# Hybrid decoder step, second mixer: level evictions, level 0's exponentials and the eviction of value tiles take other places in the order

## The chip, the cores and the metric

The kernel runs on one core of a Trainium2 chip. The metric is the device time of one execution in microseconds (us), lower being better; the median of three runs is given. Inside the core, TensorE (PE) does the matmuls, VectorE (DVE) and ScalarE (ACT) the elementwise work, GpSimd (POOL) a few side tasks, and SyncE (SP) issues the DMA transfers. Each engine runs its own list of instructions strictly in the order in which the program writes them, and engines wait for each other by semaphores (`wait_ge`).

## The reference

Two layers over 544 tokens: a prompt of 512 tokens and 8 sampled sequences of 4 tokens, with 1024 features. Each layer is a half-step feed-forward block, a token mixer, another half-step feed-forward block and a gated embedding. Layer 0 mixes by GLA with 4 heads, layer 1 by HGRN2 with 8 heads; the second one is what changes here:

```python
def hgrn2_mixer(u, w_in, gn, w_out, lb, s0):
    z = u @ w_in
    q, f, i, g = jnp.split(z, cuts, axis=-1)
    q = jax.nn.silu(q)
    log_f = jnp.logaddexp(jnp.log(lb), jnp.log1p(-lb) + jax.nn.log_sigmoid(f))
    k = (1.0 - lb) * jax.nn.sigmoid(-f)
    o, s = chunked_gated_linear_recurrence(heads(q), heads(k), heads(i), heads(log_f), s0, 1.0)
    o = rms_norm(o, gn) * jax.nn.silu(heads(g))
    return o.reshape(B, T, HGRN_I_DIM) @ w_out, s
```

```python
attn = jnp.einsum('bthk,bshk,btshk->bhts', qc, kc, decay) * scale     # pairwise decay, s <= t
o_intra = jnp.einsum('bhts,bshv->bthv', attn, vc)
o_inter = jnp.einsum('bthk,bhkv->bthv', qc * jnp.exp(b), S) * scale
```

## The kernel before, in words

Weights come in units of 512 KB, through a ring of 4 slots (`w_raw`). ACT rounds a unit to its high part (`high`, L1136), DVE subtracts to get the low part (`low`, L1677), and PE multiplies high by high, high by low and low by high. `ahead(n)` on ACT and DVE prepares unit n + 2 while PE works on unit n. SP may load a slot again only when the unit in it is free; the units of the values are also read raw by `sample_values`, so the unit behind them waits for that too.

A mixer is worked in two groups of heads, one after the other. For the second mixer these are groups 2 and 3, of 4 heads each, and the steps of one group are:

- **features**: 8 tiles, keys j = 0 to 3 and queries j = 4 to 7, evicted by DVE (`head_out`). Behind them ACT and DVE make the gate: `gate_end` on DVE (L2141) leaves the log decay in `gate_sum` (G). The queries in Q get their swish on ACT (`queries`, L1377), heads 0 to 2 ahead of the unit that follows j = 7, and head 3 behind it.
- **steps**: PE runs gate tile g0 and the diagonal products `diagonal` (L804, which wait until both calls of `queries` are through: `q_made`), value unit v0, level 0, v1, level 1, v2, level 2, v3, level 3, gate tile g1, levels 4 and 5, gate tile g2 and level 6. The value units (L773) accumulate over v0 to v3 in four banks, one for each token tile.
- **levels**: the decayed attention inside a chunk of 128 is built from 7 levels of blocks of 1, 2, 4 ... 64 tokens. For level l DVE makes the differences of gates (`level_diffs`, L2031), ACT their exponential (L1424, `level_keys` on ACT) and the queries' one (L1408, `level_queries` on ACT), DVE the products with keys (L2059) and queries (L2087), PE the level's matmuls (`level`, L828), and DVE copies the result out of PSUM under a mask (`level_out`, L2010). `level_gates` (L2043) then adds up the gates for the next level. Levels 0 to 4 use the same PSUM banks, so PE's level l waits for the copy of level l - 1.
- **values**: ACT evicts the value tiles 0 to 3 and the samples' tile 4 with the row scale (`values_out`, L1386 and L1389). PE's g1 waits for tiles 0 and 1, its level 5 for tile 4, its g2 for all.
- **mix**: DVE multiplies the keys by their decay (L2165, `kdec_made`), SP then loads the second half of the samples' states, and PE's `sq` matmuls (L902) wait for these states.

What sets the order is only the order of the code of each engine. On PE the two waits that matter read:

```python
pe.wait_ge(s["q_made"], 2 * (gi - 1))                # diagonal
elif NH == 4 and l < 5: pe.wait_ge(s["lvl_out"], n)  # level
```

Of the kernel before, what the change touches and what calls it, by code (L numbers as in the profile page):

```python
# [154 lines left out]
def _build(nc, a, o, ctx):  # L155
# [99 lines left out]
    def gain_row(e):  # L255
# [12 lines left out]
        "lb_done gk_mm x_out x_made gate_abs gate_exp gate_ln ls_made c_made kx_made gd_made gd_abs gd_exp "  # L268
        "gd_ln k_made gate_made q_made kt_zero wup_zero k0_made diff_made ek_made eq_made kt_made qt_made lvl_mm lvl_out "
        "diag_mm diag_out xs_made vs_mm sdiag_out slvl_out chunk_exp qin_made ksuf_made ksuf_exp kdec_made dec_made "  # L270
        "kd_turned kds_turned vec_turned vec_made kd_out u_mm s_made kmask_made us_mm snew_made o_mm os_mm "
        "sq_mm sq_out ks_made seqmask_made os_out o_out osq_made var_mm var_ln ors_made og_pre og_silu og_made og_made_p out_hi out_lo ple_t ple_sig "
        "p_turned p_feat p_hi p_lo p_out ple_mm ple_x u_free y_even y_made y_turned ssq_turned y_out_a y_out_v"
    ).split()
    s = {n: ctx.enter_context(nc.semaphore(n)) for n in names}
# [278 lines left out]
    def _(pe):  # L554
# [205 lines left out]
        def values(gr, u, n):  # L760

            unit_ready(n)
            if u % 2:
                sample_values(gr, u, n)
            for c in range(4):
                if u == 0 and c == 0:
                    pe.wait_ge(s["feat_out"], gr.feat0 + gr.nfeat + 1)
                if u == 0 and c == 2 and gr.has_r:
                    pe.wait_ge(s["x_out"], 2)
                for k in range(2):  # L770
                    kk = 2 * u + k
                    for part, (x, w) in enumerate(((UH, WH), (UL, WH), (UH, WL))):
                        mm = pe.matmul(ps[:, V_BANKS[c], :], x[:, kk, c * P:(c + 1) * P], w[:, n % RING, k * 512:(k + 1) * 512],  # L773
                                       start=(kk == 0 and part == 0), stop=(kk == KT_D - 1 and part == 2))
            mm.then_inc(s["mm_units"], 1)

        def sample_values(gr, u, n):
# [347 lines left out]
    def _(act):  # L1125
# [207 lines left out]
        def features(gr):  # L1333
            n = gr.start
            for j in range(gr.nfeat):
                ahead(n)
                if j == 0 and gr.g == 0:
                    norm(gr.norm, True)
                if not gr.gla and j == 4:
                    gate(gr)  # L1340
                if not gr.gla and j == 6:
                    gate_end(gr)
                if not gr.gla and j == 7:
                    queries(gr, 0, 3)
                if gr.gi == 1 and j == 0:
                    gate(gr)
                n += 1
            if gr.gi == 0:
                gate(gr)
            for kind, j, levels in gr.steps[:-2]:  # L1350
                ahead(n)
                n += 1
                for lv in levels:
                    if lv == "diag":
                        if not gr.gla:
                            queries(gr, 3, 4)
                        level_queries(gr, 0)
                    elif lv and lv < 4:
                        level_keys(gr, lv)
                        level_queries(gr, lv)  # L1360
            level_keys(gr, 4)
            level_queries(gr, 4)
            values_out(gr, (0, 1))
            level_keys(gr, 5)
            level_queries(gr, 5)
            values_out(gr, (4, 2, 3))
            ahead(n)
            level_keys(gr, 6)
            level_queries(gr, 6)
            ahead(n + 1)  # L1370

        def queries(gr, h0, h1):

            act.wait_ge(s["feat_out"], gr.feat0 + 4 + h1)
            parts = [Q[:, h0 * T_PROMPT:h1 * T_PROMPT], Q[:, 4 * T_PROMPT + h0 * T_SAMPLE:4 * T_PROMPT + h1 * T_SAMPLE]]
            for q in parts:
                ins = act.activation(q, q, ACT.Silu)  # L1377
            ins.then_inc(s["q_made"], 1)

        def values_out(gr, tiles):  # L1380

            act.wait_ge(s["mm_units"], gr.v_unit + 4)
            act.wait_ge(s["rstd_done"], gr.norm + 1)
            for c in tiles:
                if c < 4:
                    ins = act.activation(V[:, c, :], ps[:, V_BANKS[c], :], ACT.Copy, scale=rstdT[:, c:c + 1])  # L1386
                else:
                    act.wait_ge(s["vs_mm"], 2 * gr.gi + 2)
                    act.activation(V[:, c, 0:P], ps[:, V_BANKS[c], 0:P], ACT.Copy, scale=rstdT[:, c:c + 1])  # L1389
                    for j in range(1, 4):  # L1390
                        rows = slice(32 * j, 32 * j + 32)
                        ins = act.activation(V[0:T_SAMPLE, c, j * P:(j + 1) * P], ps[rows, V_BANKS[c], 0:P], ACT.Copy,
                                             scale=rstdT[rows, c:c + 1])
                ins.then_inc(s["v_out"], 1)
# [277 lines left out]
    def _(dve):  # L1672
# [235 lines left out]
        def features(gr):  # L1908
            n = gr.start
            qs = [(Q, h, gr.q_scale if gr.gla else None) for h in range(gr.NH)]  # L1910
            ks = [(K, h, None) for h in range(gr.NH)]
            dests = ([(RT, None, None)] if gr.has_r else []) + (qs + ks if gr.gla else ks + qs)
            if gr.gi == 1:

                dve.wait_ge(s["x_out"], 4)
                dve.tensor_copy(halves(G[:, 0:2 * T_PROMPT]), OG[:, 6:8, 0:T_PROMPT])
                dve.tensor_copy(halves(samples(G, gr)), OG[:, 6:8, T_PROMPT:T]).then_inc(s["x_made"], 1)
                dve.wait_ge(s["x_made"], 1)
            for j, (dst, h, scale) in enumerate(dests):
                if not gr.gla and j == 5:  # L1920
                    log_sigmoid(gr)
                    gate(gr)
                    head_out(gr, j, n, dst, h, scale)
                    gate_diff(gr)
                    ahead(n)
                    gate_key(gr)
                    n += 1
                    continue
                if not gr.gla and j == 7:
                    gate_end(gr)  # L1930
                ahead(n)
                if gr.gi == 1 and j == 1:
                    log_sigmoid(gr)
                if gr.g == 1 and j == 0:
                    dve.wait_ge(s["og_made"], 2 * gr.gi)
                    dve.wait_ge(s["og_made_p"], 2 * gr.gi)
                if h is None:
                    feature_out(gr, j, n, dst)
                else:
                    head_out(gr, j, n, dst, h, scale)  # L1940
                n += 1
                if gr.g == 0 and j == 1:
                    sample_tokens(gr)
                if gr.g == 1 and j in (0, 2):
                    sequences(GROUPS[gr.gi - 1], j // 2)
                if gr.has_r and j >= gr.nfeat - 2:
                    gates_out(gr, range(2) if j == gr.nfeat - 2 else (2,))
            if gr.gi == 0:
                log_sigmoid(gr)
            for kind, j, levels in gr.steps[:-2]:  # L1950
                ahead(n)
                n += 1
                for lv in levels:
                    if lv == "diag":
                        if gr.gla:
                            level_gates(gr, 0)
                        feature_out(gr, gr.nfeat, n - 1, OG[:, 4 * gr.g, :])
                        if not gr.gla:
                            level_queries(gr, 0)
                            level_gates(gr, 0)  # L1960
                        if gr.has_r:
                            gates_out(gr, (3,))
                        diagonal(gr)
                        level_diffs(gr, 1)
                    elif lv and lv < 4:
                        level(gr, lv)
                        level_out(gr, lv - 1)
            level(gr, 4)
            level_out(gr, 3)
            level(gr, 5)  # L1970
            ahead(n)
            feature_out(gr, gr.nfeat + 1, n, OG[:, 4 * gr.g + 1, :])
            level_out(gr, 4)
            level_keys(gr, 6)
            if not gr.gla:
                level_queries(gr, 6)
            level_gates(gr, 6)
            if gr.gla:
                ahead(n + 1)
            else:  # L1980
                feature_out(gr, gr.nfeat + 2, gr.g3_unit - 1, OG[:, 4 * gr.g + 2, :])
# [78 lines left out]
                                        compact(DK, gr, L, r), ALU.mult)  # L2060
            ins.then_inc(s["kt_made"], 1)

        def level(gr, l):

            level_keys(gr, l)
            if not gr.gla:
                level_queries(gr, l)
            level_gates(gr, l)
            level_diffs(gr, l + 1)

        def level_queries(gr, l):

# [434 lines left out]
```

## Time and profile before

| | |
|---|---|
| median of three runs | 2236.64 us (2236.31 to 2238.49) |
| the profiled execution's own time | 2235.69 us |
| its span, first to last instruction | 2233.3 us |
| TensorE busy | 2213.9 us, 99% of the span |
| DVE, ACT, POOL busy | 1577.2 us, 1083.9 us, 332.3 us |
| granted TensorE clock, mean | 0.997 |

The span is what the rows below are read in; 2.4 us of the execution's own time lie outside it, and the median of the runs is 0.95 us above the profiled execution. A busy PE means that some matmul was in flight, so its gaps are the waits of PE, and a gap is what a change of order can take away or add.

### The profile page before, as it was taken

How to read it: one execution, taken by the hardware profiler on the slowest of the kernel's cores; microseconds unless marked ns; L12 is line 12 of the kernel's file. 1: busy time of each engine (PE TensorE's matmuls, PEld its weight loads, DVE VectorE, ACT ScalarE, POOL GpSimd, SP SyncE). 2: the span in 40 equal slices, each digit the busy share in tenths (PEclk: the TensorE clock that was granted, in tenths of full speed). 3: DMA queues.
4: the chain of work that ended last, by engine and by line, in shares of the span. 5: the costliest groups of instructions: out<-in, count | busy, mean ns of one | idle time of the engine just before them, and what ended most of it. 6: DMA issues, size and time to landing. Idle time of an engine off the chain costs nothing. (4 is left out here: it accounts for less than half of the span.)

```text
span 2233.3 us, 42317 instructions
## 1 busy us (share of the span) xinstructions
PE 2213.9 (99%) x17778; PEld 2168.5 (97%) x17778; DVE 1577.2 (71%) x2172; ACT 1083.9 (49%) x1573; POOL 332.3 (15%) x239
## 2 busy tenths in 40 slices
PE   9999999999999999999999999999999999999998
PEld 8999999989999999999999999998999999999998
DVE  7888833567678888535788884359688788886344
ACT  7555622443555555423655562255465565555234
POOL 3222101112111221000222210000000212220001
PEclk9999999999999999999999999999999999999999
DMA  4333333233352333333233333322333333333231
GB/s 136 102 107 95 102 100 83 58 105 93 102 137 76 107 102 102 91 102 86 67 110 99 95 100 95 105 71 67 91 95 105 104 91 95 111 97 107 83 96 49
DMA packets 387338, 213.36 MB, mean 96 GB/s; under 512 B 7007, under 2 KB 381438, under 8 KB 387150
## 3 DMA queue, kind: packets, MB, share of 16 engines
q1 hardware_dynamic: 386928, 210.59, 33.6%
q8 instruction: 140, 2.29, 0.4%
q14 instruction: 48, 0.39, 0.1%
q10 hardware_dynamic: 190, 0.05, 0.0%
q0 software_dynamic: 32, 0.03, 0.0%
HBM read 198.98 MB, written 11.67 MB: 94 GB/s over the span
## 5 line engine op out<-in xcount | busy, mean ns | idle before, releaser
L642 PE MATMUL ps<-u_diffs,w_high 128*128 128x272 f32 x2560 | 486.8, 288 | 2.3 <-DVE w_low L1773 1.7
L642 PEld LDWEIGHTS ps<-u_diffs,w_high 128*128 128x128 f32 x2560 | 402.1, 188 | 3.2 <-issue 3.0
L642 PE MATMUL ps<-u_diffs,w_low 128*128 128x272 f32 x1280 | 369.3, 289 | 0.0
L1677 DVE TENSOR_TENSOR w_low<-w_raw,w_high 128x1024 fp32r<-128x1024 f32 x205 | 259.1, 1281 | 98.1 <-ACT w_high L1136 97.8
L2399 POOL TENSOR_TENSOR hidden<-t_gate,t_up 128x544 f32<-128x544 f32 x84 | 190.1, 2263 | 717.7 <-ACT t_gate L1258 717.7
L570 PE MATMUL ps<-hid_high,w_high 128*128 128x272 f32 x1408 | 290.4, 287 | 0.0
L570 PE MATMUL ps<-hid_high,w_low 128*128 128x272 f32 x1408 | 289.5, 288 | 0.0
L570 PE MATMUL ps<-hid_low,w_high 128*128 128x272 f32 x1408 | 289.1, 287 | 0.0
L642 PE MATMUL ps<-u_high,w_low 128*128 128x272 f32 x960 | 277.5, 289 | 0.0
L642 PE MATMUL ps<-u_low,w_high 128*128 128x272 f32 x960 | 276.9, 288 | 0.0
L642 PE MATMUL ps<-u_high,w_high 128*128 128x272 f32 x960 | 275.9, 287 | 0.3 <-DVE w_low L1773 0.3
L1136 ACT ACTIVATE w_high<-w_raw 128x1024 fp32r<-128x1024 f32 x205 | 210.4, 1049 | 113.4 <-PE ps L570 73.6
L570 PE MATMUL ps<-u_high,w_high 128*128 128x272 f32 (+2 forms) x1168 | 245.7, 292 | 2.2 <-DVE u_low L1690 1.8
L642 PEld LDWEIGHTS ps<-u_diffs,w_low 128*128 128x128 f32 x1280 | 240.6, 188 | 0.0
L570 PE MATMUL ps<-u_high,w_low 128*128 128x272 f32 (+2 forms) x1168 | 240.4, 288 | 0.0
L570 PE MATMUL ps<-u_low,w_high 128*128 128x272 f32 (+2 forms) x1168 | 240.3, 287 | 0.0
L1773 DVE TENSOR_TENSOR w_low<-w_sums,w_high 128x512 fp32r<-128x512 f32 (+1 forms) x240 | 208.6, 869 | 21.5 <-ACT w_high L1227 20.5
L570 PEld LDWEIGHTS ps<-hid_low,w_high 128*128 128x128 f32 x1408 | 220.1, 188 | 0.0
L570 PEld LDWEIGHTS ps<-hid_high,w_low 128*128 128x128 f32 x1408 | 219.3, 188 | 0.0
L570 PEld LDWEIGHTS ps<-hid_high,w_high 128*128 128x128 f32 x1408 | 219.2, 188 | 0.0
L1161 ACT ACTIVATE u_high<-h_resid,vectors 128x544 fp32r<-128x544 f32 x48 | 36.1, 751 | 372.7 <-DVE h_resid L1873 322.3
L570 PEld LDWEIGHTS ps<-u_high,w_high 128*128 128x128 f32 x1168 | 184.1, 188 | 5.6 <-DVE u_low L1690 2.4
(292 smaller groups left out, 4093.7 us busy)
## 6 DMA issues: line engine op xcount, KB each, us to landing
w_raw<-in_ffn_w_gu_dram SPq DMA_DIRECT2D x176, 512.0 KB, 5.2
w_raw<-in_ffn_w_down_dram SPq DMA_DIRECT2D x64, 512.0 KB, 4.5
w_raw<-in_hgrn_w_in_dram SPq DMA_DIRECT2D x32, 512.0 KB, 4.7
w_raw<-in_gla_w_in_dram SPq DMA_DIRECT2D x25, 512.0 KB, 5.0
w_raw<-in_ffn_w_down_dram SPq DMA_DIRECT2D x32, 384.0 KB, 4.5
w_raw<-in_ple_w_gate_dram SPq DMA_DIRECT2D x16, 512.0 KB, 4.9
states_s<-in_state_gla_dram SPq DMA_DIRECT2D x8, 512.0 KB, 5.9
out_gla_s_dram<-states_s SPq DMA_DIRECT2D x8, 512.0 KB, 3.8
```

The costliest lines, as they stand in the source:

```text
L570: mm = pe.matmul(ps[:, bank + hf, 0:t1 - t0], weights(slot, w0 + k, wk, m0, P, kw), x[:, kk - w0, t0:t1], start=(kk == 0 and part == 0), s ...
L642: mm = pe.matmul(ps[:, bank, 0:HALF], half_slot(w, base, h)[:, k * P:(k + 1) * P], x(k), start=start and k == 0 and part == 0, stop=k == K ...
L1136: act.activation(WH[:, slot, :], RAW[:, slot, :], ACT.Copy).then_inc(s["hi_made"], 1)
L1161: act.activation(flat_of(UH, m), flat_of(H, m), ACT.Copy, scale=gain_of(e, m)).then_inc(s["uh_done"], 1)
L1677: dve.tensor_tensor(WL[:, slot, :], RAW[:, slot, :], WH[:, slot, :].bitcast(F32), ALU.subtract)\
L1773: dve.tensor_tensor(half_slot(WL, base, h, n), src, half_slot(WH, base, h, n).bitcast(F32), ALU.subtract)\
L2399: pool.tensor_tensor(HID[:, f, :], tG[:, :], tU[:, :], ALU.mult).then_inc(s["hid_mul"], 1)
```

## The change

On DVE, for the second mixer: level 0's gate sums and level 1's differences are issued behind the last query tile, ahead of the weights' low part, the gate tile's eviction and the diagonal's. `level_out` of level l - 1 stands ahead of `level_gates` of level l, where it stood behind `level_diffs` of level l + 1. On ACT, for the second mixer: level 0's exponentials and its copy of the keys are issued ahead of the queries' swish, and value tiles 0 and 1 are evicted ahead of level 4's exponentials. On PE: a new semaphore `v_mm` is raised behind token tiles 0 and 1 of the last value unit, and ACT's eviction of these two tiles waits for it, in both mixers, where it waited for the whole unit. No instruction that computes is added or removed.

```diff
@@ values (PE) @@
+                if u == 3 and c < 2:
+                    mm.then_inc(s["v_mm"], 1)
             mm.then_inc(s["mm_units"], 1)
@@ features (ACT) @@
                 if not gr.gla and j == 7:
+                    level_queries(gr, 0)
                     queries(gr, 0, 3)
...
                     if lv == "diag":
-                        if not gr.gla:
+                        if gr.gla:
+                            level_queries(gr, 0)
+                        else:
                             queries(gr, 3, 4)
-                        level_queries(gr, 0)
...
+            if not gr.gla:
+                values_out(gr, (0, 1))
             level_keys(gr, 4)
             level_queries(gr, 4)
-            values_out(gr, (0, 1))
+            if gr.gla:
+                values_out(gr, (0, 1))
@@ values_out (ACT) @@
-            act.wait_ge(s["mm_units"], gr.v_unit + 4)
             act.wait_ge(s["rstd_done"], gr.norm + 1)
             for c in tiles:
+                if c < 2:
+                    act.wait_ge(s["v_mm"], 2 * gr.gi + c + 1)
+                else:
+                    act.wait_ge(s["mm_units"], gr.v_unit + 4)
@@ features (DVE) @@
                     head_out(gr, j, n, dst, h, scale)
+                if not gr.gla and j == 7:
+                    level_gates(gr, 0)
+                    level_diffs(gr, 1)
...
                             level_queries(gr, 0)
-                            level_gates(gr, 0)
...
                         diagonal(gr)
-                        level_diffs(gr, 1)
+                        if gr.gla:
+                            level_diffs(gr, 1)
                     elif lv and lv < 4:
                         level(gr, lv)
-                        level_out(gr, lv - 1)
             level(gr, 4)
-            level_out(gr, 3)
-            level(gr, 5)
+            level(gr, 5, False)
@@ level (DVE) @@
-        def level(gr, l):
+        def level(gr, l, out=True):
             level_keys(gr, l)
             if not gr.gla:
                 level_queries(gr, l)
+                if out:
+                    level_out(gr, l - 1)
             level_gates(gr, l)
             level_diffs(gr, l + 1)
+            if gr.gla and out:
+                level_out(gr, l - 1)
```

On ACT, group 2, from the unit's high part behind j = 7 to the keys' exponential of level 1 (`q<-q` is the swish, `ex<-gate_sum` and `k_tilde<-k` are level 0's exponentials and copy), before:

```order
L1136 ACTIVATE w_high<-w_raw 128x1024
L1377 ACT_TABLE_LOAD
L1377 ACTIVATE q<-q 128x1536
L1377 ACTIVATE q<-q 128x96
L1136 ACTIVATE w_high<-w_raw 128x1024
L1377 ACTIVATE q<-q 128x512
L1377 ACTIVATE q<-q 128x32
L1406 ACT_TABLE_LOAD
L1406 ACTIVATE ex<-gate_sum 128x64
L1408 ACTIVATE ex<-gate_sum 128x8x64 x2
L1416 ACTIVATE k_tilde<-k 128x512 x2
L1136 ACTIVATE w_high<-w_raw 128x1024 x2
```

and now, in the same place (lines have moved by 2 to 10):

```order
L1138 ACTIVATE w_high<-w_raw 128x1024
L1416 ACTIVATE ex<-gate_sum 128x64
L1418 ACTIVATE ex<-gate_sum 128x8x64 x2
L1426 ACTIVATE k_tilde<-k 128x512 x2
L1384 ACT_TABLE_LOAD
L1384 ACTIVATE q<-q 128x1536
L1384 ACTIVATE q<-q 128x96
L1138 ACTIVATE w_high<-w_raw 128x1024
L1384 ACTIVATE q<-q 128x512
L1384 ACTIVATE q<-q 128x32
L1138 ACTIVATE w_high<-w_raw 128x1024 x2
L1434 ACT_TABLE_LOAD
```

The three groups of level 0 moved ahead of the swish; the number of table loads is the same, and the second one now stands ahead of level 1's exponential.

On DVE, group 2, levels 3 and 4 (`w_low` is a unit's low part, `k_tilde` and `q_tilde` the level's keys and queries, `gate_sum` the gate sums, `ex` the next level's differences, `attn` the copy under the mask), before:

```order
L1677 TENSOR_TENSOR w_low<-w_raw,w_high 128x1024
L2059 TENSOR_TENSOR k_tilde<-k,ex 128x64x8 x2
L2087 TENSOR_TENSOR q_tilde<-q,ex 128x8x64 x2
L2043 TENSOR_TENSOR gate_sum<-gate_sum 128x8x8x8 x2
L2031 TENSOR_TENSOR ex<-gate_sum 128x8x64 x2
L2010 COPY_PREDICATED attn<-masks,ps 128x8x16x4 x2
L2059 TENSOR_TENSOR k_tilde<-k,ex 128x32x16 x2
```

and now:

```order
L1687 TENSOR_TENSOR w_low<-w_raw,w_high 128x1024
L2070 TENSOR_TENSOR k_tilde<-k,ex 128x64x8 x2
L2102 TENSOR_TENSOR q_tilde<-q,ex 128x8x64 x2
L2021 COPY_PREDICATED attn<-masks,ps 128x8x16x4 x2
L2054 TENSOR_TENSOR gate_sum<-gate_sum 128x8x8x8 x2
L2042 TENSOR_TENSOR ex<-gate_sum 128x8x64 x2
L2070 TENSOR_TENSOR k_tilde<-k,ex 128x32x16 x2
```

The copy moved two places up, so that the differences of level 4 now stand directly ahead of the keys of level 4, which need the exponential of these differences.

## Rows read from the trace of the kernel before

**Rows 1.** The page's busy times: engine, busy us, share of span, instructions.
```profile
PE 2213.9 (99%) x17778; PEld 2168.5 (97%) x17778; DVE 1577.2 (71%) x2172; ACT 1083.9 (49%) x1573; POOL 332.3 (15%) x239
```

**Rows 2.** Waits of PE over the whole span: total us, times, longest.
```profile
PE ps L828 <- DVE attn L2010: 2.8, 4, 1.0
```

**Rows 3.** Timeline of PE, group 2: start, duration, instruction, idle before and releaser.
```profile
1512.52 3.73 PE L804 MATMUL ps<-q,k 128*128 128x128 f32 x32
...
1530.43 0.40 PE L773 MATMUL ps<-w_low,u_high 128*128 128x512 f32 x1
1531.84 2.02 PE L828 MATMUL ps<-q_tilde,k_tilde 128*128 128x128 f32 x16 [1.01 <-DVE attn L2010]
...
1539.57 0.40 PE L773 MATMUL ps<-w_low,u_high 128*128 128x512 f32 x1
1540.36 2.02 PE L828 MATMUL ps<-q_tilde,k_tilde 128*128 128x128 f32 x16 [0.40 <-DVE attn L2010]
...
1556.75 3.73 PE L828 MATMUL ps<-q_tilde,k_tilde 128*128 128x128 f32 x32
...
1581.62 1.96 PE L902 MATMUL ps<-states_s,q 128*32 128x128 f32 x64 [0.27 <-issue]
```

**Rows 4.** Timeline of ACT, group 2.
```profile
1506.66 1.04 ACT L1136 ACTIVATE w_high<-w_raw 128x1024 fp32r<-128x1024 f32 x1
1507.72 1.28 ACT L1377 ACT_TABLE_LOAD   x1
...
1511.53 0.73 ACT L1377 ACTIVATE q<-q 128x512 f32<-128x512 f32 x2
...
1513.57 0.26 ACT L1406 ACTIVATE ex<-gate_sum 128x64 f32<-128x64 f32 x1
...
1516.02 1.99 ACT L1136 ACTIVATE w_high<-w_raw 128x1024 fp32r<-128x1024 f32 x2
...
1529.82 1.06 ACT L1136 ACTIVATE w_high<-w_raw 128x1024 fp32r<-128x1024 f32 x1 [6.06 <-DMA w_raw<-in_hgrn_w_in_dram]
...
1552.62 1.06 ACT L1424 ACTIVATE ex<-ex 128x1024 f32<-128x1024 f32 x1 [2.17 <-DVE ex L2031]
1553.58 1.14 ACT L1408 ACTIVATE ex<-gate_sum 128x512 f32<-128x512 f32 x2
1554.98 1.11 ACT L1392 ACTIVATE v_tok<-ps,rstd_tok 32x128 f32<-32x128 f32 x3
```

**Rows 5.** Timeline of DVE, group 2.
```profile
1504.96 3.39 DVE L2141 SCALAR_TENSOR_TENSOR gate_sum<-gate_sum,lbd,gate_tmp 128x512 f32<-128x512 f32 x8 [1.08 <-ACT gate_tmp L1463]
...
1537.71 2.50 DVE L2010 COPY_PREDICATED attn<-masks,ps 128x512 f32<-128x512 uint32 x2
...
1552.50 1.33 DVE L2010 COPY_PREDICATED attn<-masks,ps 128x512 f32<-128x512 uint32 x2
1553.81 1.29 DVE L2059 TENSOR_TENSOR k_tilde<-k,ex 128x512 f32<-128x512 f32 x2
1555.02 1.28 DVE L2087 TENSOR_TENSOR q_tilde<-q,ex 128x512 f32<-128x512 f32 x2
1556.23 1.28 DVE L2043 TENSOR_TENSOR gate_sum<-gate_sum 128x512 f32<-128x512 f32 x2
1557.55 1.29 DVE L2031 TENSOR_TENSOR ex<-gate_sum 128x512 f32<-128x512 f32 x2
1558.76 1.22 DVE L1677 TENSOR_TENSOR w_low<-w_raw,w_high 128x1024 fp32r<-128x1024 f32 x1
...
1566.51 0.72 DVE L1881 TENSOR_TENSOR out_gate<-ps,rstd 128x544 f32<-128x544 f32 x1 [1.06 <-PE ps L570]
...
1571.83 2.49 DVE L2165 TENSOR_TENSOR k<-k,ex 128x1024 f32<-128x1024 f32 x2
```

**Rows 6.** Waits of SP's queue, 1565 to 1590 us.
```profile
SPq L477 <- DVE k L2165: 4.0, 1, 4.0
```

**Rows 7.** Windows, PE in the first mixer: stretch, its us, busy, granted clock.
```profile
598.00:603.00 5.00, 5.00 (x23) 0.66 0.00 0
```

More of the change, by code:

```diff
@@ L270, in _build @@
         "diag_mm diag_out xs_made vs_mm sdiag_out slvl_out chunk_exp qin_made ksuf_made ksuf_exp kdec_made dec_made "
-        "kd_turned kds_turned vec_turned vec_made kd_out u_mm s_made kmask_made us_mm snew_made o_mm os_mm "
+        "kd_turned kds_turned vec_turned vec_made kd_out u_mm v_mm s_made kmask_made us_mm snew_made o_mm os_mm "
         "sq_mm sq_out ks_made seqmask_made os_out o_out osq_made var_mm var_ln ors_made og_pre og_silu og_made og_made_p out_hi out_lo ple_t ple_sig "
```

## The prediction

> **What bounds the kernel now.** I read the page's busy times first. PE is busy for 99% of the span [rows 1], so the time is PE's work plus its few waits, and off PE's path a shorter wait is worth nothing. Then PE's waits: the only ones in the second mixer that this change is near are the four ahead of the levels' matmuls (L828), which wait for DVE's masked copies (L2010), 2.8 us in all [rows 2]. The timeline of PE in group 2 shows two of them, 1.01 us ahead of level 1 and 0.40 us ahead of level 2 [rows 3]; four waits in two groups that run the same code make the other two group 3's. The reader is to see what a wait really costs: the matmuls of v1 start 0.23 us apart, so behind the one at 1530.43 level 1 could start at 1530.66 and started at 1531.84, 1.18 us late; behind the one at 1539.57 level 2 started at 1540.36 where 1539.80 was possible, 0.56 us late. That is 1.74 us a group, 3.5 us for both: the most that the change can win on this path, 0.16% of the time.
>
> Then I followed what PE waits for just ahead of that, whether or not it waits long: the diagonal (L804) needs both swish calls (`q_made`). On ACT the last swish starts at 1511.53 and takes 0.73, so ends at 1512.26 [rows 4]; PE's diagonal starts at 1512.52 [rows 3]. No idle time is shown there, but the slack is 0.26 us and no more.
>
> **The change, part by part.** I take group 2 and write its schedule on with the durations of the rows. A handover between DVE and ACT takes some 0.04 us; from DVE to PE it is 0.15.
>
> *Swish later.* On ACT, the unit's high part at 1506.66 ends at 1507.70. There the table load and the swish followed; now level 0's exponentials come first. They need the gate: DVE's L2141 group starts at 1504.96 and takes 3.39, to 1508.35 [rows 5]. So ACT idles for 0.7 us, to 1508.39, and then does the exponentials and the key copy, which took from 1513.57 to 1516.02, 2.45 us [rows 4]. Everything up to the last swish moves by 0.69 + 2.45 = 3.14, and `q_made` comes at 1515.40. No cover: PE has issued g0 and stands at the diagonal, with 0.26 us of slack. With the handover it starts at 1515.55, **3.0 us later than before**. Behind PE's waiting instruction stands all of PE's work, so the whole of it moves.
>
> *DVE's sums earlier, copies earlier.* With PE 3.0 us later, level 1 can start at 1530.66 + 3.03 = 1533.69. DVE now has 2.7 us less to do ahead of the copy of level 0 (gates and differences at 1.3 each [rows 5], the samples' small ones aside), and a PE that comes later: the copy ends about 1530, and PE doesn't wait. Level 2 could start 7.9 us after level 1, at 1541.6; what DVE needs for it is below, and it is ready at about 1540. So both old waits go: the balance at level 2 is 1541.6 against 1540.36, **+1.2 us**.
>
> *What is late next: levels 4 and 5.* DVE is held at one place by a transfer. The high part of g1's weights waited for its DMA until 1529.82 [rows 4]; SP may only issue it when `sample_values` of v1 is through, so it moves with PE, to 1532.85, the high part ends at 1533.91, and DVE's low part starts at 1533.95. From there I add starts on DVE [rows 5]: low part 1.15; level 2's keys 1.2, queries 1.2, copy 2.45, gates 1.3, differences 1.2; low part 1.2; level 3's five the same but with a copy of 1.3, 6.2. That is 1549.85. Before, the copy stood between the differences of level 4 and the keys of level 4, and it covered the time that ACT takes for the exponential between them (1.06 us, L1424 [rows 4]). Now nothing stands there: DVE waits 1.2 us (1.06, two handovers and the tail of the differences). Level 4 6.2, again a wait of 1.2, keys and queries of level 5 2.5: 1560.95 to 1561.05. Levels 1 to 3 don't show this bubble, since the next unit's low part stands in the same place. PE reaches level 5 half of its 3.73 us behind the start at 1556.75 [rows 3], moved by 1.2, so at 1559.7, and starts at 1561.2: **+1.45 us**. ACT gives the same figure: value tile 4, which level 5 needs too, comes behind the exponentials of level 5, which start at 1557.5; exponentials 2.0 and tile 1.4 end it at 1560.9.
>
> *Value tiles one by one.* Tiles 0 and 1 now go out while PE still does tiles 2 and 3. ACT has them done before level 4's differences reach it, so this costs nothing; it wins nothing either, since PE's g1 shows no wait for them before. In the first mixer only the semaphore changes, and PE shows no idle row in its levels there.
>
> *The states.* From the gates of level 5 to the end of the keys' decay, before, DVE took from 1556.23 to 1574.32, with 1.06 us idle [rows 5]: 17.0 us of work. Now it starts at 1561.0 and has no idle time left: 1578.1, 3.8 us later. SP loads the second half of the states behind that (its 4.0 us wait for L2165 [rows 6]), and PE's L902, which needs them, started at 1581.62, behind an idle of 0.27 us put down to "issue" [rows 3]. I take this to be the landing, 7.3 us behind the keys' decay. It comes at 1585.4 now, while PE, moved by 1.2 + 1.45 and about 0.2 more at level 6, would be there at 1584.3. So **+0.9 us**, and group 2 ends 3.8 us later. If the landing is not what held L902, this term is nothing.
>
> *Sum.* Group 2 gives +3.8. Group 3 runs the same code; I have no row of a wait at its L902, so its landing came up to 0.3 us earlier, and I take +3.6, between 3.0 without that term and 3.8. Together **+7.4 us**: the profiled execution's span of 2233.3 becomes 2240.7, its own time of 2235.69 becomes 2243.1, and the median, 0.95 above that execution, 2244.0. PE has no later wait in which this could vanish: its remaining waits are for copies and sums that move with it.
>
> *The clock.* In the first mixer, from 598 to 603, the granted clock is 0.66 on average, one fall to half (1.2 GHz) and back, behind a stretch of small matmuls with no idle row [rows 7]. It takes 5.0 x 0.34 = 1.7 us of clock. The wait at the diagonal is three times the longest one that the second mixer now has. The Trainium skill (TensorE: Matmul & The Clock Gate, "Why this matters for your kernels") advises against long gaps between bursts of matmuls, since an idle PE falls back to half its clock; by that rule each diagonal would bring a slow stretch. The trace does not show it for a gap of this length, only the fall in the first mixer. By the row the sum stays at 2244.0; by the rule it would be 3.4 more.
>
> **The rivals.** *The clock falls behind the diagonal's wait* in one or both groups: 2245.7 or 2247.4. For it: the fall of [rows 7] needed no idle row at all. Against: the waits of 1.01 us cost none, and the work on both sides is dense. *Only the swish counts*: DVE keeps up better than I add up (the transfer of g1 lands early, or the bubble is filled), levels 5 and 6 and the states cost nothing, and each group ends 1.2 us later: 2239.0, within what can be told from no change. For it: the added terms stand on a chain of some 25 starts, and 1.4 us of slack would hide them. Against: each start is a row. *The swish is not late*, the other side: the change does what its order suggests, the two waits go and nothing comes, -3.5 us, 2233.1. This needs `q_made` to be at most 0.26 us later than before. It decides on the 0.7 + 2.45 us on ACT; it turns into a loss when ACT's delay passes 0.26 + 1.74 = 2.0 us. Against it: both figures are rows, and ACT went from the high part into the swish's table load without a gap [rows 4], so there is no idle time in front of it to fill. *The change doesn't do what it says*: the copies wait for PE's level 0 anyway, so moving them up is worth less than their 2.7 us; but with PE late the old waits go in any case, so this leaves the sum as it is.
>
> **How the numbers follow.** A measurement of this kernel can tell about 0.2%, 4.5 us, from no change, so faster begins at 2232.2 and slower at 2241.1. My forecast with its near variants (2242 to 2245): 0.55. The clock in one or both groups: 0.20. Only the swish: 0.14. The swish not late: 0.06, of which a third ends beyond 0.2%. Something between: 0.05. So slower 0.79 (0.55 + 0.20 and most of what lies between), same 0.18, faster 0.03. Likeliest 2244.0; the range for 8 in 10 reaches down to the case of the swish alone and up to both slow stretches: 2238.8 to 2248.0. The likeliest case's own range is 2242 to 2246.
>
> **What would show it.** Right: PE idle for about 2.8 us ahead of the diagonal in both groups, released by ACT's swish; no wait for L2010 ahead of levels 1 and 2; a wait of about 1.3 us ahead of level 5, released by the queries or value tile 4; DVE idle for 1.2 us ahead of the keys of levels 4 and 5; L902 up to 1 us late behind its states. Wrong: a diagonal without a wait, which would throw the whole sum; or the diagonal's wait with none ahead of level 5, which leaves +1.2 us a group. A stretch of half clock behind the diagonal would show the first rival.

## The result and the profile after

| | before | after |
|---|---|---|
| median | 2236.47 us (2235.13 to 2238.49, 6 runs) | 2245.4 us (2242.05 to 2247.53, 6 runs) |
| profiled execution, own time | 2235.69 us | 2245.68 us |
| its span | 2233.3 us | 2243.9 us |

The ratio is 1.0038, 95% interval 1.0027 to 1.0048: slower by 8.9 us, clear of the 0.2% that can be told. The forecast was 2244.0, with 2238.8 to 2248.0 for 8 in 10. Of all executions on record one, in the second set of runs of the changed kernel, was slow throughout (2389.57 us at a mean granted clock of 0.85), and no figure below holds it.

The timeline of PE after, with the places that answer to [rows 3]: the diagonal, levels 1, 2, 4 and 5 and the states' matmuls of group 2, then diagonal, level 5 and states of group 3:

```profile
1515.33 5.43 PE L806 MATMUL ps<-q,k 128*128 128x128 f32 x32 [2.93 <-issue]
...
1535.18 1.95 PE L830 MATMUL ps<-q_tilde,k_tilde 128*128 128x128 f32 x16
...
1543.07 1.95 PE L830 MATMUL ps<-q_tilde,k_tilde 128*128 128x128 f32 x16
...
1559.38 1.95 PE L830 MATMUL ps<-q_tilde,k_tilde 128*128 128x128 f32 x16
1562.62 2.02 PE L830 MATMUL ps<-q_tilde,k_tilde 128*128 128x128 f32 x16 [1.30 <-DVE q_tilde L2102]
...
1586.89 1.95 PE L904 MATMUL ps<-states_s,q 128*32 128x128 f32 x64 [1.16 <-issue]
...
1660.50 3.81 PE L806 MATMUL ps<-q,k 128*128 128x128 f32 x32 [2.90 <-issue]
...
1706.36 2.02 PE L830 MATMUL ps<-q_tilde,k_tilde 128*128 128x128 f32 x16 [1.49 <-DVE q_tilde L2102]
...
1729.92 1.96 PE L904 MATMUL ps<-states_s,q 128*32 128x128 f32 x64 [0.45 <-issue]
```

The diagonal now has 2.93 and 2.90 us of idle time in front of it, where it had none. Levels 1 and 2 start without a wait. Level 5 waits for DVE's queries, and L904 (L902 before) waits in both groups. The diagonal of group 2 also takes 5.43 us for what takes 3.81 in group 3: the clock.

```profile
1510.00:1525.00 15.00, 12.07 (x72) 0.89 0.00 1
1655.00:1670.00 15.00, 12.10 (x80) 1.00 0.01 1
```

These are windows of PE after (stretch, its us, busy, granted clock, DMA share, GB/s), 15 us around the two diagonals: the first has a stretch at half clock, the second has none, with the same idle time.

The changed kernel was profiled once more later. Its rows of the diagonal, level 5 and the states in both groups:

```profile
1515.24 5.33 PE L806 MATMUL ps<-q,k 128*128 128x128 f32 x32 [2.92 <-issue]
...
1562.30 2.02 PE L830 MATMUL ps<-q_tilde,k_tilde 128*128 128x128 f32 x16 [1.16 <-DVE q_tilde L2102]
...
1586.26 1.96 PE L904 MATMUL ps<-states_s,q 128*32 128x128 f32 x64 [0.86 <-issue]
...
1659.84 3.81 PE L806 MATMUL ps<-q,k 128*128 128x128 f32 x32 [2.88 <-issue]
...
1705.52 2.02 PE L830 MATMUL ps<-q_tilde,k_tilde 128*128 128x128 f32 x16 [1.30 <-DVE q_tilde L2102]
...
1728.58 1.95 PE L904 MATMUL ps<-states_s,q 128*32 128x128 f32 x64
```

The diagonals are as in the first profile, the slow first one included, and level 5 waits in both groups; but group 3's states are waited for in the first profile only.

The timeline of ACT after, which answers to [rows 4]:

```profile
1506.38 1.05 ACT L1138 ACTIVATE w_high<-w_raw 128x1024 fp32r<-128x1024 f32 x1
1508.12 0.26 ACT L1416 ACTIVATE ex<-gate_sum 128x64 f32<-128x64 f32 x1 [0.68 <-DVE gate_sum L2156]
...
1510.69 1.28 ACT L1384 ACT_TABLE_LOAD   x1
...
1514.50 0.73 ACT L1384 ACTIVATE q<-q 128x512 f32<-128x512 f32 x2
...
1534.21 1.06 ACT L1138 ACTIVATE w_high<-w_raw 128x1024 fp32r<-128x1024 f32 x1 [13.40 <-DMA w_raw<-in_hgrn_w_in_dram]
```

The reader is to see the wait of 0.68 us for the gate, and that the swish's table load comes 4.3 us behind the start of the high part, where it came 1.06 behind it. The last swish ends at 1515.23 and PE's diagonal starts at 1515.33: so I take "issue" in PE's row to be this semaphore; a run further down, with less idle time there, names it (`<-ACT q L1386`).

The timeline of DVE after, which answers to [rows 5]:

```profile
1504.68 3.40 DVE L2156 SCALAR_TENSOR_TENSOR gate_sum<-gate_sum,lbd,gate_tmp 128x512 f32<-128x512 f32 x8 [1.08 <-ACT gate_tmp L1473]
...
1552.57 1.29 DVE L2070 TENSOR_TENSOR k_tilde<-k,ex 128x512 f32<-128x512 f32 x2 [1.22 <-ACT ex L1434]
...
1560.03 1.29 DVE L2070 TENSOR_TENSOR k_tilde<-k,ex 128x512 f32<-128x512 f32 x2 [1.23 <-ACT ex L1434]
1561.24 1.29 DVE L2102 TENSOR_TENSOR q_tilde<-q,ex 128x512 f32<-128x512 f32 x2
...
1571.58 0.73 DVE L1891 TENSOR_TENSOR out_gate<-ps,rstd 128x544 f32<-128x544 f32 x1
...
1576.89 2.50 DVE L2180 TENSOR_TENSOR k<-k,ex 128x1024 f32<-128x1024 f32 x2
```

The two bubbles ahead of the keys of levels 4 and 5 are there, 1.22 and 1.23 us; the idle time that DVE had ahead of the gate tile's eviction is used up; the keys' decay ends at 1579.39, where it ended at 1574.32.

### The profile page after: what moved, and what is told of

The parts are those of the page before. It is cut to its first block, busy times and chain, and to the rows that moved or that the text cites. A ratio compares the mean times of both kernels' runs of the same rounds, so it can differ in the third digit from the quotient of the medians.

```text
span 2243.9 us, 42317 instructions
## 1 busy us (share of the span) xinstructions
PE 2216.8 (99%) x17778; PEld 2172.0 (97%) x17778; DVE 1575.7 (70%) x2172; ACT 1084.5 (48%) x1573; POOL 332.7 (15%) x239
## 4 chain that ended last, share of the span: by engine, by line
PE 93%; DVE 3%; ACT 2%; issue 1%; DMA 0%; POOL 0%; DVEq 0%; ACTq 0%; SPq 0%
PE ps L570 46%; PE ps L642 37%; PE ps L773 3%; PE ps L830 1%; PE ps L890 1%; PE ps L806 1%; PE ps L924 1%; PE ps L871 1%; PE ps L956 0%; DVE attn L2021 0%; DMA w_raw<-in_hgrn_w_in_dram 0%; PE ps L970 0%; DVE w_low L1783 0%; DVE ex L2042 0%; PE ps L940 0%
```

## The experiments

Three theories stand in the expectations. A is that of the prediction: the late swish, the gap that the copies left open, and the states behind them. B: the swish is the whole loss. C: the early copies are. Each set of runs stands beside runs of the kernel before on the same chip. To compare places across runs that start a little apart, I count from the start of DVE's gate end (the L2141 group of [rows 5]) of the same group to the diagonal and to L902, and from group 2's gate end to the first matmul of the output projection. Times that a run's own clock falls add are in these numbers.

| kernel | ratio to before, 95% interval | group 2: diagonal, L902 | group 3: diagonal, L902 | to projection |
|---|---|---|---|---|
| before | 1 | 7.56, 76.66 | 7.57, 76.33 | 230.18 |
| changed | 1.0038 (1.0027, 1.0048) | 10.65, 82.21 | 10.63, 80.05 | 239.46 |
| swish first | 1.0023 (1.0014, 1.0033) | 7.55, 78.18 | 7.59, 77.59 | 234.59 |
| level 0 alone | 1.0036 (1.0023, 1.0048) | 10.65, 80.13 | 10.65, 78.74 | 238.81 |
| copies 2, 3 late | 1.0020 (1.0011, 1.0028) | 10.61, 80.09 | 10.61, 77.59 | 236.53 |
| both repairs | 0.9993 (0.9984, 1.0002) | 7.56, 75.70 | 7.59, 75.79 | 230.30 |
| states split | 1.0042 (1.0030, 1.0055) | 10.63, 79.06 | 10.60, 80.90 | 237.15 |
| wait filled (12) | 1.0029 (1.0018, 1.0041) | 10.60, 79.40 | 10.59, 80.29 | 236.88 |
| changed, second set | 1.0035 (1.0024, 1.0046) | 10.63, 81.65 | 10.61, 79.35 | 239.81 |
| both repairs, states split | 0.9997 (0.9989, 1.0006) | 7.56, 75.43 | 7.58, 75.75 | 229.38 |
| tiles together | 1.0055 (1.0041, 1.0069) | 10.62, 81.62 | 10.63, 80.36 | 240.81 |
| tiles together, second set | 1.0043 (1.0029, 1.0057) | 10.62, 81.89 | 10.61, 82.32 | 242.19 |
| tiles together, wait filled | 1.0027 (1.0016, 1.0039) | 10.59, 79.99 | 10.59, 80.11 | 237.31 |

**Swish first.** The changed kernel with level 0's exponentials and sums put back:

```diff
 # ACT, features
-                    level_queries(gr, 0)
                     queries(gr, 0, 3)
...
-                        if gr.gla:
-                            level_queries(gr, 0)
-                        else:
+                        if not gr.gla:
                             queries(gr, 3, 4)
+                        level_queries(gr, 0)
 # DVE, features: level_gates(gr, 0) and level_diffs(gr, 1) back to their old places
```

> The changed kernel with level 0's exponentials and sums put back behind the swish, on ACT and DVE; the early copies and the single value tiles stay. Theory A (the swish made late costs 3.0 us a group, the copies moved out of the gap ahead of the keys' exponentials cost a wait ahead of level 5, and DVE's lateness delays the states): no wait ahead of the diagonal, none for the copies ahead of levels 1 and 2, but some 2.2 us ahead of level 5 of each group and L902 late by up to 1 us; +1.5 us a group, about 2239.5. Theory B (the swish is the whole loss, and the rest of the change wins what it aims at): 2233, no wait ahead of level 5. Theory C (the early copies are the loss, the swish costs little): 2243 or more.

Measured: 2241.36 us (2239.72 to 2243.9, 9 runs), and these waits of PE in the second mixer (total us, times, longest):

```profile
PE ps L830 <- DVE q_tilde L2097: 4.9, 2, 2.6
PE ps L904 <- issue: 0.9, 1, 0.9
```

No wait for the copies and none at the diagonal, but 2.30 and 2.60 us ahead of level 5. So the early copies (the single value tiles were left in as well) cost time with nothing late in front of them: theory B falls. So does C: the diagonal starts 3.1 us earlier than in the changed kernel, and the median is 4 us lower. To L902, it is 1.5 and 1.3 us later than before, as forecast for each group; the median is 1.9 us above the forecast, and its profile has a fall of the clock late in group 2's mix that the profile of before does not have there.

**Level 0 alone.** The kernel before with only the lines that the previous run takes back; copies and tiles as before.

> The kernel before with only one part of the change, level 0's exponentials and sums ahead of the swish, on ACT and DVE; copies and value tiles as before. Theory A: 2.9 us of idle time ahead of both diagonals, the wait ahead of level 1 gone, one of about 1 us ahead of level 2, none ahead of level 5; +2.4 us a group, about 2241.3, and up to 1.7 us more for each group whose diagonal meets half clock. Theory B: the same loss as the whole change and more, 2245 or above. Theory C: 2236 or below, no wait ahead of the diagonal.

Measured: 2245.03 us (2241.86 to 2246.55, 5 runs).

```profile
PE ps L805 <- issue: 5.8, 2, 2.9
PE ps L829 <- DVE attn L2014: 1.6, 2, 0.9
```

The waits are those of theory A: 2.9 us ahead of each diagonal, the wait ahead of level 1 gone, 0.72 and 0.89 us left ahead of level 2, none ahead of level 5. To L902, group 3, which shows no fall at its diagonal, is 2.4 us later than before. The median, 8.5 us above before, is what theory B had said, but the waits aren't B's: the profiled execution shows half clock at the first diagonal and late in both mixes. The median doesn't settle it. The profiled execution took 2242.34 us, 2.7 below the median, and holds some 4.3 us of waits up to L902 (3.47 + 2.41, less 1.56 for the slow diagonal); where the other executions lost their time no profile shows. And the wait ahead of level 2 is longer than before (0.40 and 0.38): PE coming late took away level 1's wait, not level 2's. That one needs the early copy.

**Copies of levels 2 and 3 late.**

```diff
 def level(gr, l, out=True):
     level_keys(gr, l)
     if not gr.gla:
         level_queries(gr, l)
-        if out:
+        if l - 1 in (0, 1):
             level_out(gr, l - 1)
     level_gates(gr, l)
     level_diffs(gr, l + 1)
-    if gr.gla and out:
+    if out and (gr.gla or l - 1 not in (0, 1)):
         level_out(gr, l - 1)
```

> The changed kernel with the copies of levels 2 and 3 alone put back behind the differences, where they cover the keys' exponentials of levels 4 and 5. Theory A: 2.9 us ahead of the diagonals as in the changed kernel, nothing ahead of levels 1 to 6, no idle time of DVE ahead of the keys of levels 4 and 5; about 3 us faster than the changed kernel: +1.5 us a group over the kernel before, 2239.5, and up to 1.7 us more for each diagonal at half clock. Theory B: no gain over the changed kernel's 2245. Theory C: 2236 to 2237.

Measured: 2241.32 us (2239.1 to 2242.94, 11 runs).

```profile
PE ps L807 <- issue: 5.8, 2, 2.9
PE ps L905 <- issue: 0.5, 1, 0.5
```

Putting two copies back takes 4 us off the changed kernel: the waits ahead of level 5 are gone, and of L902's 0.54 us are left in group 2 and none in group 3. The copies were cover, not only work.

**Both repairs.** The edits of the first and the third run together.

> Both repairs: level 0 back behind the swish, only the copies of levels 0 and 1 early, the value tiles single. Theory A: no wait ahead of the diagonal and of levels 1, 2 and 5, about 0.6 us ahead of level 3 of each group (its copy of level 2 is now the late one); -1 us a group, about 2234.6, 0.1% faster than the kernel before. Theory B: the same as with all copies early, 2233. Theory C: 2236 to 2239, no gain.

Measured: 2235.06 us (2231.75 to 2237.32, 11 runs) beside 2236.55 us before.

```profile
PE ps L831 <- DVE attn L2017: 1.8, 2, 1.1
```

The one wait of the levels that is left is ahead of level 3, 0.75 and 1.08 us. To L902 both groups are faster than before, by 0.96 and 0.54 us; behind it this execution has a fall of the clock late in group 2's mix, so that the projection starts no earlier (230.30 against 230.18). The interval of the ratio, 0.9984 to 1.0002, just holds 1: a gain of 1.5 us is likely and not proved.

**States split.** The second half of the samples' states in two steps:

```diff
-                    sp.wait_ge(s["kdec_made"], N_KD[gr.gi + 1])
+                    for part in range(2):
+                        sp.wait_ge(s["kdec_made"], N_KD[gr.gi] + part + 1)
+                        # two sequences of all heads each
```

> The changed kernel, with the second half of the samples' states loaded in two steps, the first behind the first part of the keys' decay and the second behind the second, where all of it waited for the second. If the landing of the states is what holds L902 (1.16 and 0.45 us in the changed kernel), these waits shrink by 0.5 to 1.2 us in the first group and go in the second; 1 to 1.5 us below the changed kernel, about 2244.2. If they wait for something else, both stay and the time is 2245.4.

Measured: 2246.06 us (2241.93 to 2249.37, 5 runs). The diagonals and the states' matmuls (L911 here) in the profile:

```profile
1515.33 3.81 PE L813 MATMUL ps<-q,k 128*128 128x128 f32 x32 [2.91 <-issue]
...
1583.76 1.96 PE L911 MATMUL ps<-states_s,q 128*32 128x128 f32 x64
...
1657.34 5.20 PE L813 MATMUL ps<-q,k 128*128 128x128 f32 x32 [2.88 <-issue]
...
1727.64 1.95 PE L911 MATMUL ps<-states_s,q 128*32 128x128 f32 x64
```

No wait at the states' matmuls is left in either group; to them it takes 79.06 us in group 2, where the changed kernel took 82.21 with a fall of the clock worth 1.62 (5.43 - 3.81), so 80.6 without. So in group 2 the landing of the states was what held L902: both profiles of the changed kernel have the wait there, 1.16 and 0.86 us. For group 3 this run shows nothing, since the second profile of the changed kernel has no wait there either, with the load unsplit. The median, forecast at 2244.2, didn't show it: the runs scatter over 7.4 us, more than the term. The same edit on top of both repairs:

> The version with both repairs (swish first, only the copies of levels 0 and 1 early) and the states loaded in two steps. Theory A: no wait at L902 in either group, 0.7 to 1.1 us ahead of level 3 as in the version without the split; 0.2 us below that version, so 2234.9, 0.07% below the kernel before, which five rounds may not tell from it.

Measured: 2235.64 us (2233.25 to 2239.35, 11 runs), ratio 0.9997 (0.9989 to 1.0006). No wait at L902, 1.8 us ahead of level 3 in all; not to be told from before or from the version without the split.

**The wait filled.** 25 matmuls of ones ahead of the diagonal's wait:

```diff
+                for i in range(25):
+                    pe.matmul(ps[:, 4, 0:P], ones[:, :], ones[:, :], start=True, stop=True)
                 pe.wait_ge(s["q_made"], 2 * (gi - 1))
```

> The changed kernel, with 25 matmuls of ones by ones (128x128, into a bank that the diagonal overwrites) that PE does ahead of its wait for the swish; their results are used by nothing. They take about 2.7 us, so they lie inside the wait of 2.9 us. Theory A with the clock (the idle time lets the clock fall behind the first diagonal, and that costs some 1.6 us): no stretch at half clock behind either diagonal, the diagonal's group of matmuls in 3.8 us in both groups, and the median 1 to 1.7 us below the changed kernel's 2245.4, so about 2244. Without a part for the clock: 2245.4, and the falls stay.

Measured: 2250.16 us (2248.17 to 2250.34, 5 runs). The size was wrong: a matmul in f32 of this shape leaves two records, and 25 took 5.74 us, not 2.7, so the diagonals started 2.5 us later still. The timeline of PE shows it:

```profile
1512.92 5.74 PE L804 MATMUL ps<-ones 128*128 128x128 f32 x50
1518.50 3.74 PE L808 MATMUL ps<-q,k 128*128 128x128 f32 x32
```

With 12 of them, and the changed kernel again on the same chip:

> As the run with 25 filling matmuls, which took 5.7 us and so held the diagonal up by 2.5 us more in each group; now 12 of them, about 2.75 us, inside the wait of 2.9 us. Their results are used by nothing. With a part for the clock (an idle PE lets it fall, a fall costs some 1.6 us): the diagonals start where they start in the changed kernel, 10.6 us behind the gate's end on DVE, no stretch at half clock begins there, and the median is 1 to 2 us below that of the changed kernel on the same chip. Without: falls and time as in the changed kernel.

> The changed kernel itself, unaltered, as the measure for the run with the filled wait and for the one with the tiles together on the same chip: 2245 to 2246; if the falls of the clock move with the chip and not with the code, up to 2 us to either side.

Measured: 2243.19 us (2241.13 to 2244.34, 6 runs) with the filled wait; 2244.4 us (2241.47 to 2247.04, 6 runs) for the changed kernel. The first diagonal with the filled wait, and the windows of PE around both:

```profile
1512.97 2.84 PE L804 MATMUL ps<-ones 128*128 128x128 f32 x24
1516.02 3.84 PE L808 MATMUL ps<-q,k 128*128 128x128 f32 x32 [0.21 <-ACT q L1386]
```

```profile
1510.00:1525.00 15.00, 14.79 (x105) 1.00 0.00 1
1655.00:1670.00 15.00, 14.84 (x120) 1.00 0.01 1
```

The diagonals start where they did (10.60 and 10.59 us), PE is busy instead of idle, and the clock stays at its upper level. In the changed kernel's own profile of that set the first diagonal again took 5.33 us. The median is 1.2 us lower although PE does more, but the intervals of the two ratios (1.0029 and 1.0035) overlap widely, so this pair of medians doesn't prove the gain.

All profiles together, those further down included, say more. With the wait open, 8 of 14 diagonals took 5.20 us or more (seven profiles, two groups each). None of the 6 diagonals behind a filled wait did (12 matmuls twice, 25 once), and none of the 8 without a wait (before, swish first, both repairs without and with the split). And the four sets of runs with the wait open, of the changed kernel and of the one with the tiles together (below), have ratios of 1.0035 to 1.0055; the same two kernels with the wait filled by 12 matmuls have 1.0029 and 1.0027. So the idle time costs twice: its length, and a stretch at half clock behind it in some executions.

**Tiles together.** The changed kernel without the single value tiles (ACT waits for the whole last value unit again, and evicts tiles 0 and 1 behind level 4's exponentials).

> The changed kernel without its third part: value tiles 0 and 1 evicted behind level 4's exponentials and when the whole unit is done, as before. Theory A: the same time as the changed kernel, 2245.4, since DVE's lateness only shows elsewhere: PE waits some 1.6 us ahead of gate tile g1, for the two tiles, in place of the 1.3 to 1.5 us ahead of level 5. If the single tiles matter on their own: slower, 2247 to 2249.

> The kernel with value tiles 0 and 1 evicted as before, once more, beside the changed kernel on the same chip. If its 2248.6 came from more falls of the clock in that set of runs and not from the tiles: within 1.5 us of the changed kernel, with the same waits of about 1.1 us ahead of gate tile g1. If the tiles matter on their own: 2 to 3 us above it again.

Measured: 2248.63 us (2245.07 to 2250.65, 5 runs), and again 2247.01 us (2245.04 to 2247.8, 5 runs) beside 2244.4 for the changed kernel. PE's waits in the first of the two:

```profile
PE ps L570 <- ACT v_tok L1388: 2.2, 2, 1.3
PE ps L902 <- issue: 1.5, 2, 0.8
```

PE waited for the tiles ahead of g1 instead of ahead of level 5, some 1.1 us a group where 1.6 was expected, and no longer in sum than in the changed kernel (2.2 against 1.30 + 1.49), yet the median was 3.2 and 2.6 us above the changed kernel's, which by the expectations speaks for the tiles. The first profile doesn't: to L902 it takes 81.62 and 80.36 us, the changed kernel 82.21 and 80.05. The second shows half clock at both diagonals. To take that part away:

> The kernel with value tiles 0 and 1 evicted as before, and the 12 filling matmuls ahead of the diagonal's wait, whose results nothing uses. Beside the run with the filled wait and single tiles (2243.19, ratio 1.0029): if the tiles on their own cost nothing, and what the run with the tiles together lost was falls of the clock at the diagonals, the ratio is 1.0025 to 1.0035 (2242 to 2244). If the tiles matter on their own, 1.004 or above (2245 and more).

Measured: 2242.34 us (2240.09 to 2243.8, 7 runs), ratio 1.0027 (1.0016 to 1.0039), beside 1.0029 for the filled wait with single tiles. With the clock kept up at the diagonals the tiles make no difference that these intervals can tell, and none of more than 0.6 us to L902 in either group. Why the two sets with the tiles together and the wait open were slower is not settled: more falls of the clock in their executions would explain it, but only the second profile has one more at its diagonals.

## Why the prediction was right, step by step

- **The swish made late: right.** `q_made` was worked out 3.14 us later and the diagonal 3.0; behind the gate's end of group 2 the last swish ends 3.25 us later (10.55 against 7.30), and the diagonals of the two groups start 3.09 and 3.06 later. The run that takes only this back has the diagonal at 7.55 again, and the run with this alone has the same 10.65. ACT's rows show the 0.68 us of idle time and, from 1508.12 to the table load at 1510.69, 2.57 us for the work put at 2.45.
- **The old waits gone: right**, but as said there not because of the copies' new place alone: with level 0 alone, and every copy where it was, the wait ahead of level 1 goes too. The prediction said that with PE late both old waits go in any case; level 2's doesn't, 0.72 and 0.89 us stay there until the copies are early as well.
- **Levels 4 and 5: right.** The bubbles were put at 1.2 us and are 1.22 and 1.23. Level 5 was put 1.45 us late; the idle rows say 1.30 and 1.49, and 1.16 and 1.30 in the second profile. Two copies back in the gap took these waits away.
- **The states: right in group 2, open in group 3.** The term was +0.9 on top of the 0.27 us that were there. The idle row says 1.16, so 0.89 more; the second profile says 0.86, so 0.59 more. The wait goes when the load is split. (The prediction's own terms give PE's arrival as 1581.35 + 2.85 = 1584.2 and a wait of 1.2 us, of which 0.9 are new; its 1584.3 beside 1585.4 hides this.) In group 3, put at some 0.75, the wait is 0.45 in one profile and none in the other.
- **The value tiles: right.** No cost and no gain was forecast; with the clock kept up none can be told. The medians with the wait open say otherwise, by 2.6 to 3.2 us, and that is not explained in full.
- **The sum: right.** Group 2 was put at +3.8: to L902 it takes 5.55 us more, of which 1.62 are the slow diagonal, so 3.9. Group 3 at +3.6: 3.72. Together 7.65 against 7.4. The second profile gives 3.47 (4.99 less 1.52) and 3.02, together 6.49: without a wait for group 3's states it ends at the 3.0 that the prediction gave for that case.
- **The clock: here the likeliest case and the first rival came true at once.** I left it out of the sum and gave it 0.20 as a rival, against it "the work on both sides is dense"; that argument didn't hold. It fell behind the first diagonal in both profiles of the changed kernel, and with PE kept busy it fell at no diagonal. The measured 8.9 us are the 6.5 to 7.65 of waits and, by difference, some 1.3 to 2.4 for the clock. The likeliest case counted no fall and the rival one or two: the measured 2245.4 lies nearer to the rival's 2245.7 for one group than to 2244.0, and one group's fall is what both profiles show at the diagonals. The Trainium skill (TensorE: Matmul & The Clock Gate, "Why this matters for your kernels") advises against long gaps between bursts of matmuls, since an idle PE falls back to half its clock; the trace agrees for the first diagonal and, in the changed kernel's two profiles, not for the second.

Of the profiled execution's 10.6 us of longer span, 9.3 lie between group 2's gate end and the output projection. At the end of the span the output transfers behind DVE's last tile, before and after, took 4.11 and 6.06 us, 1.95 more:

```profile
2227.92 1.27 DVE L2373 TENSOR_SCALAR y_tok<-ps,rstd_tok 32x1024 f32<-32x1024 f32 x1 [0.93 <-PE ps L1094]
2236.57 1.27 DVE L2388 TENSOR_SCALAR y_tok<-ps,rstd_tok 32x1024 f32<-32x1024 f32 x1 [0.62 <-PE ps L1096]
```

What else lies outside the second mixer is some 0.6 us shorter. The change alters no order there; why the last transfers took longer wasn't looked into.

## What to carry to other kernels

A producer that shows no idle time in front of its consumer can still be the next bound: look at its slack, the time from its end to its consumer's start (here 0.26 us), before anything is put ahead of it, and price what is put there whole, with the wait that it brings. An instruction that stands between a producer's hand-off and its return is cover: moving it up for the sake of its own consumer opens the gap that it filled, so move only those copies that someone waits for. Where differences are a few us, read the waits of the profile and take the clock's falls out, since medians of five runs can mistake these for the edit.

## What the runs showed of the hardware

I had not expected that some 2.9 us of idle time in front of dense work would let the granted clock fall to half (1.2 GHz) at the first of two equal places and seldom at the second: in seven profiles with the swish late and the wait open, the first diagonal took 5.33 to 5.44 us in six and 3.81 in one, the second 3.81 in five, 5.20 in one and 6.66 in one. One such stretch adds 1.5 to 1.6 us to the first diagonal; at the second it added 1.4 once and 2.9 once. Twelve matmuls that nobody needs, put into the wait (2.84 us), kept the clock up at all four diagonals that were profiled so. A 128x128 matmul in f32 leaves two records and took 0.23 us in a row of 25.
